# The triangles of a gated delta rule, inverted on VectorE one chunk to a partition

## What is computed

```
decay = exp(where(incl, gc[..., :, None] - gc[..., None, :], -inf))
kk = einsum("bhncd,bhnjd->bhncj", k, k)
m = where(strict, beta[..., :, None] * kk * decay, 0.0) + eye(C)
sol = triangular_solve(m, concat([v * beta, k * (beta * exp(gc))]), lower, unit_diagonal)
u0, w = sol[..., :dv], sol[..., dv:]
qk = einsum("bhncd,bhnjd->bhncj", q, k) * decay
# for each chunk in turn:
u = u0 - w @ state
o = (q * exp(gc)) @ state + qk @ u
state = chunk_decay * state + (k * exp(gc[-1] - gc)).T @ u
```

## Time and profile before

| | us |
|---|---|
| median of three runs | 3185.72 (3184.1 to 3193.23) |
| the profiled execution | 3187.08 |
| its span, first to last instruction | 3185.2 |
| the stage with groups (windows 420 to 1160) | 740 |

### The profile page before, as it was taken

How to read it: one execution, slowest core, us unless ns; L and a number is a source line. 1 busy time by engine, 2 the same in 40 slices (tenths; PEclk the granted TensorE clock), 3 DMA queues, 4 the chain that set the end, 5 groups by cost and what they waited for, 6 DMA issues and landing times.

```text
span 3185.2 us, 49483 instructions
## 1 busy us (share of the span) xinstructions
PE 3023.3 (95%) x20784; PEld 2852.4 (90%) x20784; DVE 2013.0 (63%) x3003; ACT 1412.3 (44%) x2380; POOL 469.7 (15%) x400
## 2 busy tenths in 40 slices
PE   6999989999989999999998899999899999999997
PEld 6999989988989889989998899999788799997885
DVE  5457564544544445455645685567788788888886
ACT  5345344453533443344433521444355555555554
POOL 0000021221312310000130000222222211112220
PEclk9999899999999999999999999999999999999998
DMA  4434322222221135445443445999899988889994
GB/s 187 172 135 158 137 90 80 80 83 79 92 79 68 53 120 185 173 159 186 153 159 134 147 158 199 332 354 362 327 367 370 349 338 322 319 331 363 356 368 151
DMA packets 92029, 659.06 MB, mean 207 GB/s; under 512 B 10488, under 2 KB 10656, under 8 KB 14176
## 3 DMA queue, kind: packets, MB, share of 16 engines
q1 hardware_dynamic: 67968, 491.81, 42.0%
q0 software_dynamic: 22688, 159.69, 13.3%
q10 hardware_dynamic: 1152, 4.40, 0.3%
HBM read 644.74 MB, written 10.50 MB: 206 GB/s over the span
## 4 chain that ended last, share of the span: by engine, by line
PE 72%; DMA 9%; DVE 9%; ACT 7%; issue 2%; POOL 0%; SPq 0%; DVEq 0%; ACTq 0%
PE PS L922 71%; DMA raw<-in_pv 4%; DMA m<-in_pun,keep 4%; DVE WL L1546 3%; DVE m L1537 3%; ACT WH L2212 2%; ACT m L2197 2%; DMA m<-in_pv,keep 1%; ACT L2197 1%; DVE m L2037 1%; PE PS L925 0%; DMA raw<-in_w_kv 0%; ACT m L2198 0%; DVE m L1540 0%; DMA raw<-in_pu 0%
## 5 line engine op out<-in xcount | busy, mean ns | idle before, releaser
L1546 DVE TENSOR_TENSOR WL<-raw,WH 128x1024 fp32r<-128x1024 f32 x804 | 992.5, 1241 | 684.1 <-ACT WH L2212 683.3
L2212 ACT CAST WH<-raw 128x1024 fp32r<-128x1024 f32 x804 | 839.2, 1046 | 577.5 <-PE PS L922 415.4
L922 PE MATMUL PS<-m_4096r,WH 128*128 128x256 f32 x5184 | 1007.6, 294 | 15.4 <-DVE m_4096r L1537 10.5
L922 PEld LDWEIGHTS PS<-m_4096r,WH 128*128 128x128 f32 x5184 | 827.3, 196 | 36.2 <-issue 12.1
L922 PE MATMUL PS<-m_4096r,WL 128*128 128x256 f32 x2592 | 744.0, 287 | 0.0
L922 PE MATMUL PS<-m_8192r,WH 128*128 128x256 f32 (+1 forms) x2560 | 560.2, 313 | 18.6 <-issue 11.2
L922 PE MATMUL PS<-WH,m_896r 128*128 128x512 f32 x1536 | 521.6, 393 | 19.9 <-DVE m_896r L2130 19.9
L922 PEld LDWEIGHTS PS<-m_4096r,WL 128*128 128x128 f32 x2592 | 507.3, 196 | 0.0
L922 PE MATMUL PS<-m 128*128 128x128 f32 (+5 forms) x2896 | 416.3, 287 | 43.5 <-ACT m L2371 13.9
L922 PEld LDWEIGHTS PS<-m 128*128 128x128 f32 (+2 forms) x2896 | 367.2, 189 | 71.1 <-ACT m L2371 16.2
L922 PEld LDWEIGHTS PS<-m_8192r,WH 128*128 128x128 f32 x2560 | 398.1, 193 | 21.3 <-issue 11.8
(11 more groups left out here) (219 smaller groups left out, 2096.2 us busy)
## 6 DMA issues: line engine op xcount, KB each, us to landing
raw<-in_pu SPq DMA_DIRECT2D x128, 1024.0 KB, 6.8
raw<-in_pv SPq DMA_DIRECT2D x128, 1024.0 KB, 8.1
raw<-in_w_qkv SPq DMA_DIRECT2D x48, 1024.0 KB, 4.8
raw<-in_w_o SPq DMA_DIRECT2D x48, 1024.0 KB, 4.8
raw<-in_w SPq DMA_DIRECT2D x40, 1024.0 KB, 4.8
raw<-in_w_z SPq DMA_DIRECT2D x32, 1024.0 KB, 4.8
raw<-in_w_kv SPq DMA_DIRECT2D x16, 1024.0 KB, 4.8
raw<-in_w_q SPq DMA_DIRECT2D x16, 1024.0 KB, 4.8
```

Of the source, the lines that this page charges most:

```text
L922: return e.matmul(o, l, x, start=start, stop=stop)
L1546: tt(WL[:, k, :], raw[:, n % NRAW, h * 1024:h * 1024 + 1024], WH[:, k, :].bitcast(F), ALU.subtract).then_inc(S["lo"], 1)
L2212: e.copy(WH[:, k, :], raw[:, n % NRAW, h * 1024:h * 1024 + 1024]).then_inc(S["hi"], 1)
```

## The change

The five doublings per group are replaced. Ahead of the groups a new stream of steps, `invert`, is drawn beside the filler, one step for every 1/0.27 = 3.7 parts:

1. `iv_turn`, `iv_product`, `iv_store`: TensorE makes k k' for all 12 heads (24 products) and two transposes of the gates. ScalarE copies them out. GpSimd sends them through scratch tensors in device memory by DMA, so that each of 96 partitions holds one triangle (64 x 64) and its gates: two stores of gates, four loads, two stores of k k' in pieces of 256 bytes, two loads of 768 KB.
2. `iv_decay`, `iv_scale`: on VectorE and ScalarE, the two diagonal 32 x 32 blocks and the lower left block, each 96 partitions by 1024.
3. `iv_step`, 31 of them: forward substitution by columns on both diagonal blocks, two VectorE instructions each over 96 partitions and up to 512 elements, each waiting for the one before.
4. `iv_out`: VectorE writes the transpose. GpSimd stores U, T and the lower left block (six DMAs), waits for them, and clears six tiles.

`dn_load` is new too: SP loads the blocks of a group from the scratch tensors, ten DMAs of 32 partitions by 4 runs of 128 bytes, and one broadcast of the cumulative gate (128 partitions by 2 KB). For groups 0 and 1 it stands behind `iv_out`; for group g+2 it stands behind `dn_y` of group g, and waits for its last product, `o3`. SP's program therefore becomes a walk of the plan, with each weight load at the first part of the unit three before it, and the loads of a group between them.

A group keeps X (4 products) and UC (4), and W. Its steps are `dn_in`, `dn_decay`, `dn_uc`, `dn_low`, `dn_w`, the recurrence and the norm. `FILL` becomes 1.0, the first group's lead 4 instead of 8, and the order of value and gate units changes.

The core of the diff:

```
-WAITS = (1, 2, 2, 1, 1)
-FILL = 1.3
+WAITS = (1, 1, 1, 1)
+FILL = 1.0
+INV_RATE = 0.27

+    def invert(self, st):
+        self.do("iv_turn")
+        for c in range(6):
+            yield
+            self.do("iv_product", c)
+        self.do("iv_store")
+        for _ in range(4):
+            yield
+        for b in range(3):
+            self.do("iv_decay", b)
+            yield
+        for b in range(3):
+            self.do("iv_scale", b)
+            yield
+        for j in range(31):
+            self.do("iv_step", j)
+            yield
+        self.do("iv_out")
+        for g in range(2):
+            self.do("dn_load", g)
+        for _ in range(3):
+            yield

+            def dn_load(g):
+                if g < 2:
+                    s.wait_ge(*at("iv_stored", 96))
+                    s.wait_ge(*at("iv_zero", 6))
+                else:
+                    s.wait_ge(*at(f"dn_pe{g % 2}", dn_at(DN_PE, g - 2, "o3")))
...
+                for c in range(2):
+                    for b in range(2):
+                        o = 64 * c + 32 * b
+                        e.dma_start(dn_block(g, "T", o, o), t[c, b]).then_inc(ld, 16)
+                        e.dma_start(dn_block(g, "U", o, o), u[c, b]).then_inc(ld, 16)
+                    e.dma_start(dn_block(g, "BT", 64 * c, 64 * c + 32), m[c]).then_inc(ld, 16)
+                e.dma_start(dn(g, "qd"), gc_rows(g)).then_inc(ld, 16)

+            def iv_step(j):
...
+                v.step(tt(tmp, iv_u[:, :, c, j:j + 1].broadcast_to(shape),
+                          iv_e[:, 0:2, j:j + 1, r].broadcast_to(shape), ALU.mult))
+                v.own()
+                v.step(tt(iv_u[:, :, c, r], iv_u[:, :, c, r], tmp, ALU.subtract))

             def dn_in(g):
...
+                p.wait_ge(*at(f"ld_dn{g % 2}", 176 * (g // 2 + 1)))
+                for i in range(4):
+                    m = mm(blk(PS[:, bB, :], i), blk(dn(g, "BT"), i), blk(dn(g, "T"), i), True, True)
+                mark(g, "X", m)
-            def dn_x(g, l):
...
-                for i in range(4):
-                    m = mm(blk(PS[:, bB, :], i), blk(dn(g, "BT"), i), blk(dn(g, "T"), i), True, True)
-            def dn_tu(g, l):
...
-                for i in range(4):
-                    m = mm(blk(PS[:, bC, :], i), blk(dn(g, "Lb"), i), blk(dn(g, "U"), i), True, True)
+            def dn_uc(g):
+                need_a(g, "x")
+                for i in range(4):
+                    m = mm(blk(PS[:, bB, :], i), blk(dn(g, "X"), i), blk(dn(g, "U"), i), True, True)
+                mark(g, "UC", m)

+            def iv_out():
+                g_.wait_ge(*at("iv_done", 1))
+                for h in range(2):
...
+                        e.dma_start(by_chunk(scratch[name], h), x[rows, :]).then_inc(S["iv_stored"], 16)
+                g_.wait_ge(*at("iv_stored", 96))
+                for g in range(2):
+                    for name in ("T", "U", "BT"):
+                        e.tensor_copy(c4(dn(g, name)), bc(C("zero"), 4)).then_inc(S["iv_zero"], 1)
```

More of the change, by code:

```diff
@@ L64, in constants @@
     put("mt", np.where((p <= x) & same, 0.0, -BIG))
[L65 to L73, removed]
+    put("eye", np.eye(32, dtype=np.float32).reshape(1, 1024))
     put("flip", (p + x) == 127)
@@ L108, in fill_order @@
 def fill_order():
[L110 to L119, removed]
+    fill = [("v", i) for i in range(4)] + [("z", 0), ("z", 1)]
+    nv, nz = 4, 2
+    while nz < 10:
+        fill += [("v", nv), ("z", nz)]
+        nv, nz = nv + 1, nz + 1
+    fill += [("v", i) for i in range(nv, 22)]
+    nv = 22
+    while nz < 32:
+        fill.append(("z", nz))
+        nz += 1
+        if nv < 24 and nz % 2 == 0:
+            fill.append(("v", nv))
+            nv += 1
+    return fill
 FILLS = fill_order()
@@ L333, in mix @@
                 next(fz)
-        while st["v"] < 2:
+        inverse, credit = self.invert(st), 0.0
+        while not st["i"]:
             next(fz)
+            credit += INV_RATE
+            if credit >= 1:
+                credit -= 1
+                next(inverse, None)
         live, nextg, credit = [], 0, 0.0
@@ L906, in sync_program, with loads @@
                 e.dma_start(raw[:, n % NRAW, :], units[n]).then_inc(S[f"raw{n % NRAW}"], 16)
[L907 to L915, removed]
+            def loads():
+                for c in range(4):
+                    e.dma_start(quarter(MT, c), quarter(D["memT"], c)).then_inc(S[f"ld_mem{c}"], 16)
+                for n in range(NRAW):
+                    load(n)
@@ new lines, in end @@
+            def end():
+                for p in range(2):
+                    s.wait_ge(*at("out_t", 2 * p + 2))
+                    e.dma_start(out[0, tok(p), 1024:2048], OUT[p][:, 1024:2048]).then_inc(S["st_sync"], 16)
+                s.wait_ge(*at("st_sync", 32))
+                s.wait_ge(*at("st_act", 32))
+                s.wait_ge(*at("st_bias", 16))
+                s.wait_ge(*at("st_h", 16))
+                for n in range(NUNIT - NRAW, NUNIT):
+                    s.wait_ge(*at(f"raw{n % NRAW}", 16 * (n // NRAW + 1)))
@@ L918, in tensor_program @@
+            Plan({"loads": loads, "mm": unit_mm, "vm": vm, "dn_load": dn_load, "end": end}).run()
         def tensor_program(e):
```

289 lines of the change are left out of this document (161 added, 128 removed).

## The result

| | before | after |
|---|---|---|
| median of the runs, us | 3189.35 (3184.1 to 3193.23, 4 runs) | 3086.35 (3083.11 to 3092.5, 4 runs) |
| the profiled execution | 3187.08 | 3085.42 |
| first product of the output stage, us of the span | 1160.5 | 1047.8 |

What follows compares the result with a forecast made beforehand. TensorE's queue was taken to bound the stage: 474 us of products, 25 small gaps, 26 inversion, 22 hand-over and 45 group waits make 592 against 740, so 3038 us in all, range 3005 to 3065 (55%).

Steps and rivals of the forecast that it cites:

- 26 for the inversion: Inversion stretch: VectorE sets the pace by 18 us, late inputs add 8; ends 5 and 60 us.
- small gaps: Stage from 420 to 1160 us: 33 us remainder beside idle and clock, shrinking in proportion to TensorE's need, to 25.
- the slope: Substitution steps on VectorE: 1.19 ns an element and 0.08 us per instruction, 31 us for 62 instructions.
- the dear case: Substitution steps in the inversion: 62 us instead of 31, if each instruction waits as long as it runs.
- Rival 4: Inversion: the substitution is dear, 62 us instead of 31, all exposed; 3069 us in all; chance 10%.
- The late trip: Inversion inputs through device memory: chain of 18 us against 10.6 of filler, so VectorE stands about 8 us.
- The hand-over: From `iv_out` to group 0's first product: chain of 26.6 us, 7.8 covered, 2.7 of clock; 22 us, ends 5 and 45.
- The groups: From group 0 on: 316 us of TensorE's parts and rows, 26 a group, plus 45 us of group waits.
- Waits and clock: In the groups: idle and clock at the old 11% share, 35 us, plus 10, making 45; ends 15 and 100.
- Rivals 1 and 2: Group block loads: land late, 3100 us, 14%; or the eleven complete one after the other, 3269 us, slower, 5%.
- Rival 3: Inversion, hand-over and groups: waits stay hidden, VectorE ahead, chains at lower ends, groups wait 20; 2983 us; chance 13%.
- rival 5: Whole stage: TensorE's queue was not the limit, only waits moved, gain of 60 us or less; 3127 us; chance 3%.

## Why the prediction was right, and where it was off

The stage from 420 us was forecast at 592 us and took 627.8. The three windows show where the 36 us are.

**Up to the end of the inversion: 192 forecast, 196.6 measured.** The forecast is TensorE's 158, 26 for the inversion and 8 of the small gaps. TensorE waited 16.4 us for the convolution and 15.2 for ScalarE. That the sum came so near is partly luck: idle time (31.7 us) and clock (7% of 164.9, 11.5) make 43 us where I had 26, and the rows took 196.6 - 43.2 = 153 where I had 158 + 8. The steps were priced rightly:

```profile
L1800 DVE TENSOR_TENSOR m<-m,m x31: 220/548/685, 516.6 to 610.1; 96x62 f32<-96x62 f32 x2, 96x120 f32<-96x120 f32 x2, 96x174 f32<-96x174 f32 x2, 96x224 f32<-96x224 f32 x2
L1803 DVE TENSOR_TENSOR m<-m,m x31: 219/556/687, 516.8 to 610.4; 96x62 f32<-96x62 f32 x2, 96x120 f32<-96x120 f32 x2, 96x174 f32<-96x174 f32 x2, 96x224 f32<-96x224 f32 x2
```

62 at a median of 0.55 is some 34 us (the two lines sum to 16.0 + 16.2 = 32), against 31 by the slope and 62 for the dear case. Rival 4 is refuted, by the run without the steps too. The late trip was sized too small, 8 us where VectorE stood for 10.0 and TensorE for 15.2, with the clock at 0.59 and 0.81. I had seen VectorE's wait and not that ScalarE's copies out of PSUM stand in the same order behind the decay.

**The hand-over: 22 forecast, 23.9 measured.** Of the 22, 18.8 were the wait and 2.7 the clock; the clock behind it now counts in the groups. The chain that ended last, in order of time (start, length, what):

```profile
615.14 2.19 DVE m L1807
617.61 0.60 POOL s_iu L2756
...
620.36 8.71 DMA s_im<-m
629.13 3.39 POOL m L2760 x6
633.46 0.43 SPq L976
...
637.25 3.19 DMA m<-s_gb
640.48 2.09 PE PS L999 x8
```

The sum was right, 640.48 - 615.14 = 25.3 against 26.6, with parts that err both ways: the six GpSimd issues took 2.8 us and not 4.8, its clears 0.6 each and not 1.0, the stores' landing 8.7 and not 7, the eleven issues of SP 0.43 each and not 0.33, the last landing 3.2 and not 2.6. The cover was wrong: TensorE had done its 11 parts 1.5 us after `iv_out` began, so it covered 1.5 and not 7.8. The run with 15 more parts in it got 8.8 us back.

**The groups: 378 forecast, 407.3 measured.** This is the step that was furthest off, in two of its terms.
- *The small gaps.* I let 33 us shrink with the rows, to 25, of which 17 in the groups. Without idle time and clock the groups took 407.3 - 33.7 - 22.4 = 351 us where rows at 0.118 and 0.1125 and these 17 make 333. So about 18 us of the miss are slower rows, not waits. The timeline shows one place, in the products of the recurrence, which stay.

```profile
741.45 1.84 PEld L999 LDWEIGHTS PS<-m 128*128 128x128 f32 x12
...
743.41 0.30 PEld L999 LDWEIGHTS PS<-m_4096r,WH 128*128 128x128 f32 x2
...
744.32 0.41 PEld L999 LDWEIGHTS PS<-m 128*64 128x64 f32 x4
```

  From 741.45 to the next weight load at 743.41, 12 rows take 1.96 us, 0.163 each, and the four behind them, with weights 64 wide, 0.145 each (744.32 to 744.90), where X, TA and UC took 0.1125. So the rows that were removed were faster than these; what I called gaps was, at least in part, the slower pace of rows that stay. My sum had hidden it: I took 0.118 for every row of the stage before and subtracted at 0.1125. With 0.118 for the 2688 rows of filler and 0.1125 for the other 2606 the gaps of before are an estimated 48 us and not 33, and rows that stand end to end had no share in them.
- *Waits and clock.* Idle 33.7 and clock 6% of 373.6 = 22.4 make 56 where I had 45. I kept the waits at the old share of the time. The run with more products shows that rows in a group can cover such waits (38.6 of 142 us). That the doublings had done so is shown only in part. Two more waits of before, for the reciprocal (L1764) and for the copies of u (L2381):

```profile
PE PS L922 <- DVE m L1764: 5.3, 3, 3.6
...
PE PS L922 <- ACT m L2381: 4.2, 3, 2.2
```

  With the squares the norm cost 11.1 + 5.3 = 16.4 us before and costs 15.2 now; it did not grow. The waits for u did, from 4.2 to 11.4, and so did the share that the clock takes of the busy time, from 4% to 6%. ScalarE was forecast as the largest releaser there. It released 14.8 us, VectorE 16.0; the load of 65% that I worked out for ScalarE was 216/407 = 53%.

**The signs that I named.** VectorE near 9 tenths ahead of group 0: 83.6% over 100 us. TensorE idling there behind the convolution: 16.4 us. One wait of 15 to 25 us for a DMA: 24.0. Groups every 28 to 31 us: 407/12 = 33.9, missed. The output stage near 1010: 1047.8, missed. Matmul rows 19,444: 19,490.

**The rivals.** Rivals 1 and 2 (blocks late, or one after another) are refuted: the eleven small loads overlap, and land faster than I allowed:

```profile
L976 SPq DMA_DIRECT2D m<-s_it x42: 319/432/503, 640.1 to 970.7; - x42
...
DMA to landing us min/median/max: 1.5/1.8/2.0
```

1.8 us for 16 KB in runs of 128 bytes, against 9.5 for the gates' store. For group 0 the eleven loads took from the first issue at 632.6 to the last landing at 640.4, 7.8 us. The Trainium skill ("DMA: Bandwidth & Descriptors", Anatomy of one DMA) gives a fixed cost of about 2.0 us for one DMA, measured on the path through GpSimd. The trace, with loads of SP, is of that size, and it agrees with the overlapped case: 7.8 us is far from the 22 of eleven in turn. Rival 3 (waits hidden) fell with the waits of 24.0 and 15.2 us, rival 5 with a gain of 112.7 in the stage and with the run that puts the rows back. Behind the stage, as costed, nothing changed up to 2724.7, where the offset was still there.

## What to carry to other kernels

Work in a nearly full queue can be worth less than its own time, because it covers other chains (39 of the 142 us of the added products did), and what stays after a cut may be slower per instruction than what went. A long wait of one engine has to be followed through the order of the next ones: 10.0 us on VectorE became 15.2 on TensorE by way of a copy out of PSUM. Before filler is moved to a gap, count what is left for the steps behind it: filling the hand-over paid 8.8 us, and the early gates paid only when groups 0 and 1 had filler too.

## What the hardware showed

- SP's issue of a DMA with 32 partitions x 4 runs took 0.43 us, that of a plain weight load 0.33; ten such loads of 16 KB landed in 1.8 us each in the median, so by an estimate (1.8 / 0.43) about four were in flight at a time. The broadcast of 2 KB to 128 partitions was the slowest of the eleven, 3.2 us at least and 5.0 in the median.
- GpSimd's copy of 128 x 512 fp32 from a constant took 0.603 us, less than the 0.685 of VectorE's subtraction of that size with a PSUM operand. Its squares of that size (L2765) took 1.04 us in the median.
- Steps that wait each for the one before cost VectorE little more than their elements: 0.548 and 0.556 us in the median, 32 us for 62 against 31 by the slope, and 1.1 us of idle time in all in front of the second instructions.
